# First head, values' turning, weight splits and end of a two-block fp32 kernel put in another order

## The chip, the cores and the metric

The program runs on one core of one Trainium2 chip. A core has engines with instruction queues of their own: TensorE (PE) multiplies, VectorE (DVE), ScalarE (ACT) and GpSimd (POOL) do elementwise work, and SyncE (SP) issues most of the DMAs. They meet only through semaphores. The metric is device microseconds of one execution; the program of before takes 1271.08 us (median of three, 1270.89 to 1271.17). Here a change of less than about 0.2%, 2.54 us, counts as no change.

## What is computed

512 tokens of 1024 channels go through two blocks in fp32. The reference, cut to what matters (`split`, `topk` = 128, norms and short convolutions as named):

```
def first_block(x, ...):
    h = rmsnorm(x, norm_mix_g)
    bg, cg, xv, q, k, v, z, a, b, ga, gb = split(h @ w_in)
    y_a = (bg * causal_dwconv(cg * xv, conv_a_w)) @ w_a_out
    q, k, v = split(silu(causal_dwconv(concat(q, k, v), gdn_conv_w)))      # 8 heads of 128
    q, k = l2norm(q) * 128 ** -0.5, l2norm(k)
    o = gated_delta_rule_chunked(q, k, v, g, beta)                         # chunks of 64, triangular solve
    y_b = (rmsnorm(o) * gdn_norm_g * silu(z)) @ w_b_out
    x = x + (sigmoid(ga) * y_a + sigmoid(gb) * y_b) @ w_o
    x = x + conv_ffn(rmsnorm(x, norm_ffn_g), w_up, ffn_conv_w, w_down)
    return rmsnorm(x, norm_final_g)

def second_block(x, ...):
    z = rmsnorm_2(x, norm_g) @ w_in
    pv, pg, dq, dk, dv, dg, iq, ik, iw, fq, fk, fv, fg, ff = split_columns(z)
    a_out = pool_mixer(pv, pool_w, pool_scale) * silu(pg)
    b_out = dsa_mixer(dq, dk, dv, iq, ik, iw * 8 ** -0.5, topk) * silu(dg) # 6 heads of 64, 128 selected keys
    c_out = fox_mixer(fq, fk, fv, log_sigmoid(ff + fox_bf)) * silu(fg)     # 6 heads of 64, causal
    x = x + concat(a_out, b_out, c_out) @ w_out
    return rmsnorm_2(x, final_g)
```

## The kernel before

**Weights in two parts.** Every large product is made as units of 128 output channels by 512 tokens. A weight tile comes by DMA into `raw` (four buffers), ScalarE rounds it to its high part `whi` (L1329, two buffers), and another engine takes the difference as the low part `wlo` (two buffers). TensorE then runs 24 matmuls of 128x128 by 128x512 into a PSUM bank of `gb`: high by high, low by high, high by low for each of eight k (L833). The low part is made by VectorE in `split` (L1810), except for the units in `POOL_SPLITS`, where GpSimd makes it (L2756). These are units 9 to 21 of the second block's 32 input units (`Z_UNITS`). ScalarE's high part of unit n waits for the end of unit n-2 on TensorE, since `whi` has two buffers, and a unit starts when its low part is there.

**First block, first head.** While the eight units of the first delta-rule head run, TensorE's small steps of that head (triangular inverse, 32x32 and 64x64 blocks) stand between them, and VectorE follows an order written out by hand in `first_head()` (L2149 on). Its pieces are `norm_low(k)` (L2122, low part of the normed input's column block k, which the next head's units use), `split`, `rescale` (L2117), `conv` (L2107, three taps), `shuffles` with GpSimd's elementwise inverse (L1931 on VectorE, L2663 and L2666 on GpSimd), `step` (L2014 to L2026), `place_blocks` (copies of diagonal blocks `Up` and `Tp` into `Ui` and `T64`, L2001 and L2003), `xv_gate` (L2129), `turn_pairs` (L2008) and `query_sums` (L1980, L1981). `T64` is printed as `Yb` by the profile, with which it shares its memory. In later heads ScalarE makes the block copies (L1415).

**Second block.** `schedule()` (L107) is a table: for each of the 32 units and each quarter of a unit it lists the steps that stand beside TensorE's unit on every engine. Six head groups g, each of two heads, start 15 quarters apart, from quarter 28 on. For a group and one of four query tiles: scores on TensorE (L1207), `s` on VectorE (bias and row maximum, L2463), `exp` on ScalarE (L1730), `weigh`, a reciprocal on VectorE (L2471) and a scaling on ScalarE (L1738), then the transposition on TensorE (L1219). After the four tiles come the product with the values (L1229), `pv` (gating, L2486) and `low` (L2492). `turn_v(g)` (L2477) turns the group's values on VectorE; then SyncE sends them out and brings them back, in the units that `V_OUT` lists. Beside all this VectorE runs 48 rounds of the top-k selection (MAX8, L2443, and MATCH_REPLACE8, L2444), on 256, 384 or 512 columns, each query tile's last one ending in L2446, and after each unit `z_out` (L2510). GpSimd also makes the gates (L2738, L2739) and masks (L2728).

**End.** The last 128 tokens are normed in two halves: ScalarE squares (L1786), GpSimd makes the factor (L2765 to L2770), VectorE multiplies both halves by the gain (L2604) as soon as they are there, and when the factor is known VectorE scales half 0 (L2610) and ScalarE half 1 (L1790). Then the output leaves by DMA.

## Time and profile before

| | us |
|---|---|
| median of three runs | 1271.08 |
| profiled execution | 1270.91 |
| its span in the profile | 1269.2 |
| TensorE busy | 1253.5 (99%) |
| VectorE busy | 834.1 (66%) |
| ScalarE busy | 576.9 (45%) |
| GpSimd busy | 223.7 (18%) |

The span is what the profile records from the first to the last instruction; 1.71 us of the profiled execution lie outside it. TensorE has almost no idle time, so a share of busy time says nothing of where a few microseconds could go. What can be read is each single idle stretch of TensorE, who ended it, and what stood in that engine's queue in front. A row of the timeline is: start, duration, engine, line, operation, output and inputs, count, and in brackets the idle time before it and who ended it. Instructions on VectorE are recorded longer than they hold the queue, by the time in which the next one has already begun; where one follows another, the distance of two starts is what an instruction costs.

### The profile page before, as it was taken

Reading aid. Unit: us, or ns where it says so; the run is one execution under the profiler, and the core shown is the slowest. Engines: PE = TensorE matmul, PEld = TensorE weight load, DVE = VectorE, ACT = ScalarE, POOL = GpSimd, SP = SyncE. Lnnn points to the kernel's source line nnn. Section 1 sums busy time; section 2 is a strip of 40 time slices with the busy share of each in tenths; the row PEclk is TensorE's granted clock in tenths of the full one; section 3 lists DMA queues with packets and bytes.
Section 4 is the critical chain, followed back from the end, with each engine's and each line's share of the span. In section 5 each row is a group of like instructions: output and inputs, shape, how many; then the busy total and the mean of one; then the engine's idle time right before and its main releaser. Section 6 shows DMA issues by size and latency. Waiting matters only on the chain.

```text
span 1269.2 us, 20146 instructions
## 1 busy us (share of the span) xinstructions
PE 1253.5 (99%) x6633; PEld 1007.8 (79%) x6633; DVE 834.1 (66%) x1710; ACT 576.9 (45%) x1045; POOL 223.7 (18%) x476
## 2 busy tenths in 40 slices
PE   8999999999999999999999999999999999999998
PEld 6777878878788788888888888888888777777776
DVE  6978768687776853444477773367765687794743
ACT  5564544545454432223344442244445455666632
POOL 2613214032140400001300000000004124440021
PEclk9999999999999999999999999999999999999999
DMA  6245263443534534333233323433224333343221
GB/s 186 76 122 126 83 145 97 122 122 86 141 82 125 132 86 115 99 99 97 87 100 99 95 69 96 120 100 99 80 75 117 102 101 100 87 113 100 83 67 67
DMA packets 283492, 130.01 MB, mean 102 GB/s; under 512 B 77296, under 2 KB 276271, under 8 KB 283445
## 3 DMA queue, kind: packets, MB, share of 16 engines
q1 hardware_dynamic: 283445, 129.42, 37.2%
q8 instruction: 25, 0.41, 0.1%
q14 instruction: 22, 0.18, 0.0%
HBM read 119.34 MB, written 10.06 MB: 102 GB/s over the span
## 4 chain that ended last, share of the span: by engine, by line
PE 90%; DVE 4%; issue 1%; ACT 1%; POOL 0%; DVEq 0%; ACTq 0%
PE gb L833 78%; PE gb L1279 2%; PE gd L1279 1%; PE gd L1229 1%; PE gd L1219 1%; DVE wlo L1810 1%; PE gd L1207 1%; PE gd L1005 1%; PE gd L1016 1%; PE gd L925 0%; PE gd L933 0%; PE gd L994 0%; PE gd L993 0%; PE gd L1012 0%; PE gb L1207 0%
## 5 line engine op out<-in xcount | busy, mean ns | idle before, releaser
L833 PE MATMUL gb<-act_a,whi 128*128 128x512 f32 x2656 | 888.4, 398 | 0.2 <-DVE wlo L1810 0.2
L833 PEld LDWEIGHTS gb<-act_a,whi 128*128 128x128 f32 x2656 | 498.9, 188 | 111.6 <-issue 9.5
L833 PE MATMUL gb<-act_a,wlo 128*128 128x512 f32 x1408 | 549.0, 390 | 0.0
L1810 DVE TENSOR_TENSOR wlo<-raw,whi 128x1024 fp32r<-128x1024 f32 (+1 forms) x197 | 235.6, 1196 | 134.3 <-ACT whi L1329 132.3
L1329 ACT ACTIVATE whi<-raw 128x1024 fp32r<-128x1024 f32 (+1 forms) x210 | 215.9, 1028 | 216.9 <-PE gb L833 191.6
L833 PEld LDWEIGHTS gb<-act_a,wlo 128*128 128x128 f32 x1408 | 265.1, 188 | 48.4 <-issue 0.5
L833 PE MATMUL gb<-act_b,whi 128*128 128x512 f32 x432 | 152.5, 393 | 1.3 <-DVE qc L2107 1.3
L833 PEld LDWEIGHTS gb<-act_b,whi 128*128 128x128 f32 x432 | 81.1, 188 | 18.6 <-DVE qc L2107 1.8
L2711 POOL TENSOR_TENSOR zs<-zs,ca 128x512 f32<-128x512 f32 x3 | 4.2, 1396 | 321.3 <-ACT ca L1332 321.3
L833 PE MATMUL gb<-act_b,wlo 128*128 128x512 f32 x128 | 49.9, 390 | 0.0
L2666 POOL TENSOR_TENSOR Ue<-Ue,elt 128x60 f32<-128x60 f32 (+14 forms) x120 | 45.3, 377 | 9.4
L2663 POOL TENSOR_TENSOR elt<-Ti,Ue 128x60 f32<-128x60 f32 (+14 forms) x120 | 38.0, 316 | 28.4 <-DVE Ti L1931 14.1
L2676 POOL TENSOR_TENSOR rr<-ss,eps_one 128x4 f32<-128x4 f32 x8 | 1.6, 199 | 234.6 <-DVE ss L1995 234.6
L2756 POOL TENSOR_TENSOR wlo<-raw,whi 128x1024 fp32r<-128x1024 f32 x13 | 31.2, 2398 | 23.6 <-ACT whi L1329 23.6
L1424 ACT ACTIVATE ob<-gd,hc 128x128 f32<-128x128 f32 x24 | 8.8, 368 | 54.0 <-DVE Rr L2054 54.0
L2318 DVE TENSOR_TENSOR Yb<-gb,Vt 128x512 f32<-128x512 f32 x22 | 15.2, 691 | 24.9 <-PE gb L833 24.9
L2694 POOL TENSOR_TENSOR zs<-zs,ca 128x512 f32<-128x512 f32 x3 | 5.6, 1856 | 134.3 <-ACT ca L1332 134.3
L2357 DVE TENSOR_TENSOR xT<-xT,gb 128x512 f32 (+1 forms) x16 | 11.0, 687 | 27.0 <-PE gb L833 27.0
L833 PEld LDWEIGHTS gb<-act_b,wlo 128*128 128x128 f32 x128 | 24.1, 188 | 4.5
L2443 DVE MAX8 small<-selb 128x8 f32<-128x256 f32 (+2 forms) x48 | 26.5, 551 | 0.6
L2444 DVE MATCH_REPLACE8 selb<-small,selb 128x256 f32<-128x256 f32 (+2 forms) x48 | 26.0, 543 | 0.0
L2107 DVE SCALAR_TENSOR_TENSOR kc<-gb,hw,kc 128x511 f32<-128x511 f32 (+2 forms) x24 | 18.0, 748 | 7.7 <-ACT kc L1445 7.1
(487 smaller groups left out, 1497.5 us busy)
## 6 DMA issues: line engine op xcount, KB each, us to landing
raw<-in_w_in_dram SPq DMA_DIRECT2D x102, 512.0 KB, 3.5
raw<-in_w_up_dram SPq DMA_DIRECT2D x44, 512.0 KB, 3.5
raw<-in_w_down_dram SPq DMA_DIRECT2D x16, 384.0 KB, 3.1
raw<-in_w_down_dram SPq DMA_DIRECT2D x16, 320.0 KB, 3.1
raw<-in_w_a_out_dram SPq DMA_DIRECT2D x8, 512.0 KB, 3.8
raw<-in_w_b_out_dram SPq DMA_DIRECT2D x8, 512.0 KB, 3.4
raw<-in_w_o_dram SPq DMA_DIRECT2D x8, 512.0 KB, 3.4
raw<-in_w_out_dram SPq DMA_DIRECT2D x8, 512.0 KB, 3.5
```

The costliest lines, as they stand in the source:

```text
L833: ins = pe.matmul(gb[:, b, :], l, r, start=(first and m == 0), stop=(last and m == len(todo) - 1))
L1005: pe.matmul(gd[:, 3, 0:P], Ui[:, c, :], rhs, start=True, stop=True).then_inc(vn_done, 1)
L1279: ins = pe.matmul(place(c, half), l, r, start=False, stop=(i == KD - 1 and m == 2), skip_group_check=True)
L1329: sc.activation(whi[:, i % 2, 0:k * P], raw[:, i % 4, 0:k * P], ACT.Copy).then_inc(hi_ready, 1)
L1810: dve.tensor_tensor(wlo[:, i % 2, 0:k * P], raw[:, i % 4, 0:k * P], whi[:, i % 2, 0:k * P].bitcast(F32), ALU.subtract).then_inc(split_read ...
L2107: ins = dve.scalar_tensor_tensor(dst[:, a:T], gb[:, at, 0:T - a], hw[:, 4 * b + 3 - a:4 * b + 4 - a], dst[:, a:T], ALU.mult, ALU.add)
L2318: dve.tensor_tensor(scaled[s], gb[:, 2 * q + s, :], flat(Vt), ALU.mult).then_inc(up_scaled, 1)
L2443: link(dve.max(small[:, 0:8], v))
L2444: link(dve.match_replace(v, small[:, 0:8], v, TAKEN))
L2663: pool.tensor_tensor(elt[:, :, 0:n], row_at(m), Ue[:, :, m:m + 1].to_broadcast([P, TC, n]), ALU.mult).then_inc(el_used, 1)
L2666: pool.tensor_tensor(Ue[:, :, m + 1:E], Ue[:, :, m + 1:E], elt[:, :, 0:n], ALU.subtract).then_inc(el_done, 1)
L2756: pool.tensor_tensor(wlo[:, n % 2, :], raw[:, n % 4, :], whi[:, n % 2, :].bitcast(F32), ALU.subtract).then_inc(split_ready, 1)
```

## The change

Four things change, and TensorE's own 2185 instructions stay in the same order.

1. First head, VectorE: `norm_low` 0 and 1 no longer stand ahead of the third unit's split and convolution, and all eight stand later than before; `query_sums` moves ahead of `step(13)`; the four copies `Ui<-Up` leave VectorE for ScalarE (`place_blocks`, between `level(14)` and `level(15)`), the two copies of `T64` stay.
2. Second block: `turn_v(g)` for g below 5 stands five quarters of a unit earlier, and the transfers behind it one or two units earlier (`V_OUT`).
3. `POOL_SPLITS` ends six units earlier: the low parts of units 16 to 21 are made by VectorE.
4. End: half 1 is made by one instruction on VectorE when the factor is known (gain and factor together), and ScalarE scales half 0.

```diff
-V_OUT = (13, 17, 21, 25, 28, len(Z_UNITS) + 2)
+V_OUT = (12, 16, 19, 23, 27, len(Z_UNITS) + 2)
...
-        todo.setdefault(start + (7 if g < GROUPS - 1 else 10), []).append((2, ("turn_v", g)))
+        todo.setdefault(start + (2 if g < GROUPS - 1 else 10), []).append((2, ("turn_v", g)))
...
-        POOL_SPLITS = range(N_Z + 9, N_Z + 22)
+        POOL_SPLITS = range(N_Z + 9, N_Z + 16)
...
+            def place_blocks(h):
+
+                sc.wait_ge(t_ready, 3 * h + 2)
+                for b in range(P // B):
+                    ins = sc.activation(Ui[rows(b), :, rows(b)], Up[rows(b), :, :], ACT.Copy)
+                ins.then_inc(ui_ready, 1)
+
...
                 level(14)
+                place_blocks(0)
                 level(15)
...
-            sc.activation(outs[:, TC - 1, T:2 * T], outs[:, TC - 1, T:2 * T], ACT.Copy,
+            sc.activation(outs[:, TC - 1, 0:T], outs[:, TC - 1, 0:T], ACT.Copy,
                           scale=small[:, 36 + TC - 1:36 + TC]).then_inc(outs_ready, 1)
...
                 dve.wait_ge(t_ready, 3 * h + 2)
-                for b in range(P // B):
-                    dve.tensor_copy(Ui[rows(b), :, rows(b)], Up[rows(b), :, :])
                 for b in range(2):
-                    ins = dve.tensor_copy(T64[rows(b), :, rows(b)], Tp[rows(b), :, :])
-                ins.then_inc(ui_ready, 1)
+                    dve.tensor_copy(T64[rows(b), :, rows(b)], Tp[rows(b), :, :])
...
                 shuffles(range(0, 7))
-                norm_low(0)
-                norm_low(1)
                 split(N_B + 5, N_B + 5)
...
                 query_rows(0)
-                norm_low(2)
-                norm_low(3)
+                norm_low(0)
                 step(11, 0)
                 split(N_B + 7, N_B + 7)
                 step(12, 0)
                 rescale(5)
                 turn_values(0)
+                query_sums(0)
                 step(13, 0)
                 place_blocks(0)
                 xv_gate(0)
+                norm_low(1)
+                norm_low(2)
+                turn_pairs(0)
+                norm_low(3)
                 norm_low(4)
-                turn_pairs(0)
-                query_sums(0)
-                norm_low(5)
                 split(N_B + 8, N_B + 8)
                 rescale(6)
                 filter_a(0)
                 bg_in(0)
+                norm_low(5)
                 norm_low(6)
+                first_state(0)
                 norm_low(7)
-                first_state(0)
                 rescale(7)
...
-            for half in range(2):
-                dve.wait_ge(osq, TC + half)
-                ins = dve.tensor_tensor(outs[:, TC - 1, half * T:half * T + T], gd[:, 2 + half, :],
-                                        gfin[:, half * T:half * T + T], ALU.mult)
-                if half == 0:
-                    link(ins)
-            ins.then_inc(outs_ready, 1)
+            dve.wait_ge(osq, TC)
+            dve.tensor_tensor(outs[:, TC - 1, 0:T], gd[:, 2, :], gfin[:, 0:T], ALU.mult).then_inc(outs_ready, 1)
             dve.wait_ge(orr, TC)
-            dve.tensor_scalar(outs[:, TC - 1, 0:T], outs[:, TC - 1, 0:T], small[:, 36 + TC - 1:36 + TC], None,
-                              ALU.mult).then_inc(outs_ready, 1)
+            dve.scalar_tensor_tensor(outs[:, TC - 1, T:2 * T], gd[:, 3, :], small[:, 36 + TC - 1:36 + TC], gfin[:, T:2 * T],
+                                     ALU.mult, ALU.mult).then_inc(outs_ready, 1)
```

Three places show what this does to VectorE's queue. The lines of the changed kernel stand five to eight higher for the same operation (L1810 is L1818, L2107 is L2112, L2477 is L2482). The first place is the first head, ahead of the query's convolution (`qc`). Before:

```order
88 L2122 SCALAR_TENSOR_TENSOR act_a<-Vt,par,act_a 128x512 [waits hn_hi]
89 L2122 SCALAR_TENSOR_TENSOR act_a<-gate,par,act_a 128x512 [waits hn_hi]
90 L1810 TENSOR_TENSOR wlo<-raw,whi 128x1024 [waits hi_ready]
91 L2117 TENSOR_TENSOR gb<-gb,zs 128x512 [waits unit_done,row_kept]
92 L2107 SCALAR_TENSOR_TENSOR qc<-gb,hw,qc 128x511 [waits tap_first,out_scaled]
```

and in the changed kernel:

```order
87 L1939 STREAM_SHUFFLE Ti<-Le 128x36
88 L1818 TENSOR_TENSOR wlo<-raw,whi 128x1024 [waits hi_ready]
89 L2122 TENSOR_TENSOR gb<-gb,zs 128x512 [waits unit_done,row_kept]
90 L2112 SCALAR_TENSOR_TENSOR qc<-gb,hw,qc 128x511 [waits tap_first,out_scaled]
```

Two `norm_low` have left the place in front of the split. The second place is step 13 of the same head and what follows it on VectorE. Before:

```order
121 L1990 STREAM_TRANSPOSE qc<-vc 128x512 [waits conv_silu,out_scaled]
122 L2024 TENSOR_TENSOR Up<-Up,gd 128x4x16 [waits z_done]
123 L2026 STREAM_TRANSPOSE Tp<-Up 128x128 [waits u_ready]
124 L2001 COPY Ui<-Up 32x4x32 [waits t_ready]
125 L2001 COPY Ui<-Up 32x4x32 x3
126 L2003 COPY Yb<-Tp 32x4x32 x2
127 L2129 TENSOR_TENSOR cx<-gb,cx 128x512 [waits cg_copied,unit_done]
128 L2122 SCALAR_TENSOR_TENSOR act_a<-gate,par,act_a 128x512 [waits hn_hi]
129 L2008 STREAM_TRANSPOSE Yb<-Ui 32x4x32 [waits u_ready]
```

and in the changed kernel:

```order
119 L1998 STREAM_TRANSPOSE qc<-vc 128x512 [waits conv_silu,out_scaled]
120 L1988 STREAM_TRANSPOSE Ti<-ob 128x512 [waits el_done,sq_ready]
121 L1989 TENSOR_REDUCE small<-Ti 128x4x4 [waits dve_order]
122 L2029 TENSOR_TENSOR Up<-Up,gd 128x4x16 [waits z_done]
123 L2031 STREAM_TRANSPOSE Tp<-Up 128x128 [waits u_ready]
124 L2009 COPY Yb<-Tp 32x4x32 [waits t_ready]
125 L2009 COPY Yb<-Tp 32x4x32
126 L2134 TENSOR_TENSOR cx<-gb,cx 128x512 [waits cg_copied,unit_done]
127 L2127 SCALAR_TENSOR_TENSOR act_a<-gate,par,act_a 128x512 [waits hn_hi] x2
128 L2013 STREAM_TRANSPOSE Yb<-Ui 32x4x32 [waits u_ready]
```

The sums have moved ahead of the step, four copies are gone, and one `norm_low` more stands ahead of the turning of the pairs. The third place is the second block from unit 16's split on, ahead of the reciprocal of group 2's third tile. Before:

```order
718 L2443 MAX small<-selb 128x8 [waits dve_order]
719 L2444 MATCH_REPLACE selb<-small,selb 128x384 [waits dve_order]
720 L2510 SCALAR_TENSOR_TENSOR vc<-gb,wk 128x512 [waits z_read,ot_ready,unit_done,dve_order]
721 L2471 RECIPROCAL small<-small 128x2 [waits exp_ready]
```

and in the changed kernel:

```order
716 L1818 TENSOR_TENSOR wlo<-raw,whi 128x1024 [waits split_ready,hi_ready,dve_order]
717 L2482 STREAM_TRANSPOSE past_act_b<-vraw 128x512 [waits v_put,z_read]
718 L2448 MAX small<-selb 128x8
719 L2449 MATCH_REPLACE selb<-small,selb 128x384 [waits dve_order]
720 L2515 SCALAR_TENSOR_TENSOR vc<-gb,wk 128x512 [waits z_read,ot_ready,unit_done,dve_order]
721 L2476 RECIPROCAL small<-small 128x2 [waits exp_ready]
```

A split and a turning of values stand ahead of the same reciprocal. From here to unit 21 five more splits and `turn_v(3)` are put in between the rounds in the same way, and the `turn_v(2)` that stood behind L2510 thirteen rows further down is gone from there.

## Rows read from the trace of the kernel before

**Rows 1.** TensorE's waits: engine, line, releaser, us in total, times, longest.

```profile
PE gb L833 <- DVE qc L2107: 1.3, 1, 1.3
PE gd L1219 <- ACT Yb L1738: 1.0, 1, 1.0
PE gd L977 <- issue: 0.5, 1, 0.5
```

**Rows 2.** Busy time, 1120 to 1140: PE, PEld, DVE, ACT, POOL, clock, DMA.

```profile
1120.00:1140.00 20.00, 20.00 (x100) 15.06 (x97) 18.10 (x48) 11.15 (x32) 8.34 (x5) 1.00 0.40 104
```

**Rows 3.** Timeline, VectorE and TensorE around the first long wait of the first head.

```profile
43.66 0.74 DVE L2122 SCALAR_TENSOR_TENSOR act_a<-Vt,par,act_a 128x512 fp32r<-128x512 f32 x1
45.01 1.30 DVE L1810 TENSOR_TENSOR wlo<-raw,whi 128x1024 fp32r<-128x1024 f32 x1
49.33 0.50 PE L833 MATMUL gb<-act_b,whi 128*128 128x512 f32 x1 [1.34 <-DVE qc L2107]
```

**Rows 4.** Timeline around step 13 of the first head, on VectorE, GpSimd and TensorE.

```profile
58.57 5.85 POOL L2649 TENSOR_TENSOR gate<-xT,zs 128x512 f32<-128x512 f32 x4 [2.60 <-DVE Tp L2016]
61.35 0.31 DVE L2026 STREAM_TRANSPOSE Tp<-Up 128x128 f32<-128x128 f32 x1
61.69 3.04 DVE L2001 COPY Ui<-Up 32x128 f32<-32x128 f32 x4
62.53 0.44 PE L960 MATMUL gd<-Tp,LT 32*32 32x32 f32 x16
67.00 0.65 PE L977 MATMUL gd<-Yb,LT 64*64 64x64 f32 x8 [0.50 <-issue]
66.94 0.71 DVE L1980 STREAM_TRANSPOSE Ti<-ob 128x512 f32<-128x512 f32 x1
68.28 0.74 DVE L2122 SCALAR_TENSOR_TENSOR act_a<-gate,par,act_a 128x512 fp32r<-128x512 f32 x1
```

**Rows 5.** Timeline, second head: the same block copies on ScalarE.

```profile
115.17 1.27 ACT L1415 ACTIVATE Ui<-Up 32x128 f32<-32x128 f32 x4 [3.26 <-DVE Tp L2026]
```

**Rows 6.** Timeline, second block: a split on GpSimd, and L2446 on VectorE.

```profile
1064.85 2.40 POOL L2756 TENSOR_TENSOR wlo<-raw,whi 128x1024 fp32r<-128x1024 f32 x1 [1.35 <-ACT whi L1329]
1064.95 2.45 DVE L2446 TENSOR_SCALAR selb<-selb 128x256 f32<-128x256 f32 x1
1104.64 2.32 DVE L2446 TENSOR_SCALAR selb<-selb 128x384 f32<-128x384 f32 x1
1142.67 0.43 DVE L2446 TENSOR_SCALAR selb<-selb 128x512 f32<-128x512 f32 x1
```

**Rows 7.** Timeline, third tiles of groups 1 and 2 (ScalarE, TensorE), and a turning.

```profile
1069.36 0.72 ACT L1738 ACTIVATE qc<-qc,small 128x512 f32<-128x512 f32 x1 [0.53 <-DVE small L2471]
1070.13 0.66 PE L1219 MATMUL gd<-ident,qc 128*128 128x128 f32 x4 [0.44 <-ACT qc L1738]
1094.10 1.05 ACT L1329 ACTIVATE whi<-raw 128x1024 fp32r<-128x1024 f32 x1
1096.58 0.72 ACT L1738 ACTIVATE qc<-qc,small 128x512 f32<-128x512 f32 x1 [0.28 <-DVE small L2471]
1098.57 0.60 PE L1219 MATMUL gd<-ident,qc 128*128 128x128 f32 x4
1107.48 0.70 DVE L2477 STREAM_TRANSPOSE past_act_b<-vraw 128x512 f32<-128x512 f32 x1
1108.11 0.64 DVE L2492 TENSOR_TENSOR act_a<-ca,act_a 128x512 fp32r<-128x512 f32 x1
```

**Rows 8.** Timeline, the last of the changed transpositions, and VectorE's next idle stretch.

```profile
1143.19 0.49 PE L1219 MATMUL gd<-ident,qc 128*128 128x128 f32 x3
1147.32 1.23 DVE L1810 TENSOR_TENSOR wlo<-raw,whi 128x1024 fp32r<-128x1024 f32 x1 [2.31 <-ACT whi L1329]
```

**Rows 9.** Timeline, the end of the kernel.

```profile
1264.63 0.55 POOL L2770 TENSOR_TENSOR small<-small,mhalf 128x1 f32<-128x1 f32 x1
1265.45 0.72 ACT L1790 ACTIVATE gate<-gate,small 128x512 f32<-128x512 f32 x1 [1.35 <-DVE gate L2604]
```

## The prediction, made before the changed kernel was run

> **What bounds the kernel now.** I read the table of busy times first: TensorE is busy 1253.5 of 1269.2 us, so nearly all of the time is matmul work that the change leaves alone. What an edit of this kind can move is TensorE's idle time, so the second view is the list of TensorE's waits. Apart from the start and the end it holds less than 5 us in all. The ones that lie where the change is made are the wait for the query's convolution in the first head (1.3, the timeline has 1.34), the one ahead of L977 in the same head (0.50), and two waits for a `weigh` in the second block (1.0, on `Yb`, and 0.44, on `qc`) [rows 1, 3, 4, 7]. The third view is busy time by stretch: from 1120 to 1140 TensorE is never idle, but VectorE is busy 18.10 of 20 us, while GpSimd has 8.34 [rows 2]. There VectorE does not bound the kernel, yet has hardly any room. The fourth view is the timeline there. All sums are made against the profiled execution, 1270.91; the median, 1271.08, lies 0.17 above it, which is added at the end.
>
> **First head, ahead of the query's convolution.** VectorE's two `norm_low` take from 43.66 to 45.01, 1.35 us, and stand before the split, whose input was there [rows 3]. Without them the split, the rescaling and the three taps come 1.33 earlier (I leave 0.02 for the handover), and of TensorE's wait of 1.34 nothing that matters is left: -1.33. For this the eight `norm_low` are due only when the next head starts, so that they are paid out of VectorE's idle time later; nothing waits for them in this head.
>
> **Step 13.** From here TensorE asks 1.33 earlier for everything: the product L960, at 62.53 before, could start at 61.20. What it needs is VectorE's transposition L2026, which ended at 61.66 [rows 4]. On VectorE one `norm_low` fewer stands ahead, which saves about 0.7, but part of the other gain is lost because the split before it waits for ScalarE's high part, and that comes with TensorE's clock. And `query_sums` are put in: from 66.94 to 68.28, 1.34 us [rows 4]. By my replay of VectorE's queue L2026 ends at 61.35 and TensorE, with the usual small gap, starts 0.22 late. Of the 1.33, 1.11 are left.
>
> **The turning of the pairs.** L977 waited 0.50, until 67.00 [rows 4]. Now VectorE reaches `turn_pairs` without the four copies, 3.04 us, which were that long because GpSimd's four L2649 ran at the same time. It has one `norm_low` more, 0.67, and starts 0.3 earlier. The two copies of `T64` now take over the place beside GpSimd; I give them 1.1 more than without GpSimd, from the same row (a mean of 0.76 each, where the held ones carried it). So the turning comes 3.04 + 0.3 - 0.67 - 1.1 = 1.57 earlier; the wait is gone if it comes 1.11 + 0.50 = 1.61 earlier. Practically it goes: -0.50. ScalarE's four copies take 1.27 in the second head [rows 5] and lie between 62.53 and 67.00, in 4.47 us in which ScalarE has only two short pairs of copies to do; I cost them at nothing. If that cover were gone, at most 1.27 would come back. First head: -1.33 + 0.22 - 0.50 = **-1.61**, of which I leave 0.03 for waits later in the head: -1.58. The ends for this part are -1.84 (both waits gone, no new one) and 0 (the copies on ScalarE and the held copies of `T64` eat it).
>
> Here a page of the Trainium skill has a word: GPSIMD Engine Reference, Specifications, says that VectorE shares its SBUF interfaces with GpSimd and names no other engine. The trace agrees on VectorE's side (3.04 us for four tiny copies); whether ScalarE's copies stay at 1.27 beside L2649 no row of before shows.
>
> **End.** ScalarE's scaling of half 1 started at 1265.45, since it waited for VectorE's L2604 on both halves, and ended at 1266.17. GpSimd's factor was there at 1264.63 + 0.55 = 1265.18 [rows 9]. Now VectorE's instruction on half 1 (0.70 for 128x512 with two inputs) and ScalarE's on half 0 (0.72) both start behind the factor, and the end comes at about 1266.00: -0.17. Bounds: 0, and the whole 0.27 between 1265.18 and 1265.45.
>
> **Second block, the prices.** A split costs GpSimd 2.40 us, VectorE 1.23, of which some 1.15 are its own [rows 6, 8] (records overlap by 0.07, as 1107.48, 0.70 and 1108.11 show [rows 7]). A turning of values is 0.63 in the queue [rows 7]. L2446 took 2.45 and 2.32 while GpSimd had a split and 0.43, on more columns, while it had none [rows 6]: about 1.97 come back at 1104.64, since GpSimd's split there is gone. VectorE's bill from 1094 to 1149 is then 6 x 1.15 - 1.97 = +4.9, plus a wait: unit 16's high part ends only at 1095.15 [rows 7], 0.6 after VectorE would take it up. The turnings 2 and 3 only move inside this stretch.
>
> **Who waits.** A split or turning put in front of a reciprocal (L2471) delays the `weigh` on ScalarE and then TensorE's transposition. The slack is read at each place as the distance of `weigh` and transposition. At the first, group 2's third tile, `weigh` stood at 1096.58 and the transposition at 1098.57, and where TensorE waited it came 0.77 behind (1069.36 and 1070.13): slack 1.22. In front of this reciprocal now stand the split of unit 16 with its wait (1.15 + 0.62) and `turn_v(2)` (0.63), 2.4 in all, so TensorE waits 1.22 [rows 7]. At the next place, 1109.53, VectorE has won back L2446 and the turning that stood there, but carries unit 17's split: the wait of 1.05 becomes 0.60, -0.45. Then, worked out in the same way, each time on the clock that the earlier waits have already moved: the transpositions at 1115.74 (+0.78), 1123.40 (+0.45), 1127.75 (+0.51), 1135.96 (+0.50), 1143.19 (+0.22, [rows 8]) and the score products at 1146.72 (+0.40). VectorE never has a gap in between; after that its idle 2.31 ahead of 1147.32 [rows 8] takes up the rest. Sum for units 16 to 21: 1.22 - 0.45 + 2.86 = **+3.63**. The ends are -1.05 (the old wait gone, no new one) and +5.5 (the whole bill, 4.9 + 0.6, on TensorE).
>
> **Earlier turnings 0 and 1.** `turn_v(1)` now stands ahead of the reciprocal for which TensorE already waited 0.44 [rows 7], so that its 0.63 are paid in full: +0.64 with the handover. `turn_v(0)` delays unit 9's high and low part by as much, where the slack is about 0.5: +0.15. The earlier transfers of `V_OUT` meet no due date that I can find, in SyncE's queue as little as for the weights behind them: 0.
>
> **Sum.** 1270.91 - 1.58 - 0.17 + 3.63 + 0.64 + 0.15 = 1273.58; with 0.17 to the median, **1273.8**. The change trades two waits of the first head for some nine shorter ones in the second block.
>
> **Rivals.**
>
> Rival 1, faster: VectorE has the room. It is busy 66% of the span, and six splits at half of GpSimd's price, with L2446 let go, would fit between the reciprocals if the slack at the transpositions were larger than I read it, so that none of the seven is late and the wait of 1.05 goes as well. It decides at 1098.57: TensorE has no wait there. Time: 1271.08 - 1.58 - 0.17 - 1.05 = 1268.3. For it speaks that only one of eight places had a wait before; against it, VectorE's 18.10 of 20 us [rows 2].
>
> Rival 2, no change: the meeting at 1064.95 ends the other way. L2446 began 0.10 after GpSimd's split, at 1064.85, and was held for 2.0 us [rows 6]; it stands ahead of the very reciprocal that costs TensorE 0.44 and, in the change, 0.63 more. If the moved clock lets VectorE begin first, both go: -1.08, 1272.7. The same size comes out if two of the later delays overlap better than in my serial reckoning. The Trainium skill has this under Advanced Engine Details and Errata, Mode Summary: instructions of GpSimd and two-port instructions of VectorE "will interfere/block eachother". That the blocking goes both ways is the page's; the row shows VectorE's side.
>
> Rival 3, slower still: the first head gives nothing, because the `T64` copies stay held until GpSimd is done, or because ScalarE's copies come late for L977. Then 1273.75 + 1.58 = 1275.3.
>
> Rival 4: half of the bill is hidden, since the serial reckoning puts every delay on TensorE: 1273.75 - 0.5 x 4.42 = 1271.5.
>
> **Chances.** Forecast 0.45, rival 1 0.13, rival 2 0.17, rival 3 0.10, rival 4 0.15. A measurement of this kernel can tell about 0.2% from no change, that is 1268.5 to 1273.6. The forecast lies just above the upper bound; of its 0.45 I put 0.33 above and 0.12 below. With rival 3 and a little of rival 2, slower has 0.44; faster, from rival 1, 0.13; within 0.2%, 0.43. The range leaves out rival 1 and a tail above rival 3: 1269.8 to 1275.4.
>
> **What would show it.** Right: VectorE's split of the first head's third unit starts near 43.7, TensorE's wait for L2107 is gone, a wait of some 0.2 ahead of L960; in the second block a wait of about 1.2 at the transposition near 1098, others of 0.2 to 0.8 up to 1147, and VectorE without a gap from 1105 to 1149; L2446 near 1104 at about 0.4. Wrong: TensorE's busy share of 1080 to 1160 unchanged (rival 1); L2446 near 1065 at 0.4 (rival 2); L977 waiting a microsecond (rival 3). The number would also be off if the high parts of units 16 to 21 came earlier or later than before against TensorE's clock, since each of VectorE's splits waits for one.

## The result

The changed kernel takes 1274.51 us (median of ten, 1274.32 to 1274.67) against 1271.18 for the kernel before in the same runs: +3.33 us, a ratio of 1.0026 with an interval of 1.0018 to 1.0035. It is slower, by a little more than the 0.2% that a measurement can tell (the interval begins just below it). The prediction had 1273.8 and a range of 1269.8 to 1275.4; its sign and its mechanism held, most terms of its sum came out within 0.1 to 0.3 us, and the sum was 0.7 too low.

Both traces record the same 6633 matmuls of TensorE, in the same order. So the start of any one of them can be set against the start of the same one in the trace of before. This difference is called its position below; it counts what the rows of waits leave out.

The list of TensorE's waits of the changed kernel (engine, line, releaser, us in total, times, longest) answers to [rows 1]. L1746 is the changed kernel's `weigh` on ScalarE, L1738 there its `exp`:

```profile
PE gd L1219 <- ACT qc L1746: 2.9, 4, 1.1
PE gd L1219 <- ACT Yb L1746: 1.1, 3, 0.6
...
PE gb L1207 <- ACT zs L1738: 0.4, 1, 0.4
...
PE gd L984 <- ACT Yb L1506: 0.3, 1, 0.3
...
PE gd L1169 <- ACT qc L1721: 0.2, 1, 0.2
```

Both waits of the first head (1.3 on L2107 and 0.5 ahead of L977) are gone from it. The transpositions L1219, which waited twice for 1.5 us in all, now wait seven times for 4.0. The stretch of [rows 2], in the same view (PE, PEld, DVE, ACT, POOL, clock, DMA), with that of 1080 to 1100, where the chain of new waits begins:

```profile
1080.00:1100.00 20.00, 18.90 (x93) 14.42 (x92) 14.85 (x41) 11.67 (x34) 5.76 (x6) 1.00 0.14 34
...
1120.00:1140.00 20.00, 19.32 (x95) 13.42 (x95) 19.07 (x43) 10.38 (x31) 2.78 (x2) 1.00 0.37 96
```

From 1120 to 1140 VectorE is busy for 19.07 of 20 us (18.10 before), GpSimd for 2.78 (8.34), and TensorE, which had no idle time, has 0.68; from 1080 to 1100, where it had none either, it has 1.10. TensorE's clock is 1.00 in these stretches in both kernels. The timeline of the first head, VectorE, GpSimd, ScalarE and TensorE, answers to [rows 3, 4, 5]:

```profile
43.88 1.23 DVE L1818 TENSOR_TENSOR wlo<-raw,whi 128x1024 fp32r<-128x1024 f32 x1
...
56.74 5.85 POOL L2649 TENSOR_TENSOR gate<-xT,zs 128x512 f32<-128x512 f32 x4 [1.94 <-DVE Tp L2021]
...
61.05 0.31 DVE L2031 STREAM_TRANSPOSE Tp<-Up 128x128 f32<-128x128 f32 x1
61.40 1.50 DVE L2009 COPY Yb<-Tp 32x128 f32<-32x128 f32 x2
...
61.51 0.44 PE L960 MATMUL gd<-Tp,LT 32*32 32x32 f32 x16
...
62.56 1.26 ACT L1482 ACTIVATE Ui<-Up 32x128 f32<-32x128 f32 x4
...
64.96 0.30 DVE L2013 STREAM_TRANSPOSE Yb<-Ui 32x128 f32<-32x128 f32 x1
...
65.43 0.67 PE L977 MATMUL gd<-Yb,LT 64*64 64x64 f32 x8
```

The split starts at 43.88 instead of 45.01, L960 at 61.51 instead of 62.53 and L977, without a wait, at 65.43 instead of 67.00. Of the waits of before in the second block one stands in no row above (timeline of TensorE):

```profile
1109.53 0.55 PE L1219 MATMUL gd<-ident,Yb 128*128 128x128 f32 x3 [1.05 <-ACT Yb L1738]
```

In the changed kernel they stand at these places (timeline of TensorE, units 12 to 21; answers to [rows 7, 8]):

```profile
1069.97 0.66 PE L1219 MATMUL gd<-ident,qc 128*128 128x128 f32 x4 [1.01 <-ACT qc L1746]
1099.67 0.55 PE L1219 MATMUL gd<-ident,qc 128*128 128x128 f32 x3 [1.10 <-ACT qc L1746]
1110.25 0.55 PE L1219 MATMUL gd<-ident,Yb 128*128 128x128 f32 x3 [0.61 <-ACT Yb L1746]
1117.22 0.44 PE L1219 MATMUL gd<-ident,qc 128*128 128x128 f32 x2 [0.59 <-ACT qc L1746]
1125.31 0.33 PE L1219 MATMUL gd<-ident,Yb 128*128 128x128 f32 x1 [0.15 <-ACT Yb L1746]
1130.13 0.33 PE L1219 MATMUL gd<-ident,qc 128*128 128x128 f32 x1 [0.24 <-ACT qc L1746]
1138.87 0.44 PE L1219 MATMUL gd<-ident,Yb 128*128 128x128 f32 x2 [0.29 <-ACT Yb L1746]
1150.34 1.14 PE L1207 MATMUL gb<-gate 64*128 64x128 f32 x8 [0.37 <-ACT zs L1738]
```

The transposition at 1098.57 of before, which did not wait, now stands at 1099.67 with 1.10 us of waiting, and six more places follow up to 1150, of which only the first (1110.25, before at 1109.53) waited before. VectorE's side of it, the same stretch:

```profile
1095.11 1.23 DVE L1818 TENSOR_TENSOR wlo<-raw,whi 128x1024 fp32r<-128x1024 f32 x1 [0.74 <-DVE selb L2449]
1096.26 0.70 DVE L2482 STREAM_TRANSPOSE past_act_b<-vraw 128x512 f32<-128x512 f32 x1
...
1105.53 1.23 DVE L1818 TENSOR_TENSOR wlo<-raw,whi 128x1024 fp32r<-128x1024 f32 x1 [1.01 <-ACT whi L1329]
1107.92 0.36 DVE L2451 TENSOR_SCALAR selb<-selb 128x384 f32<-128x384 f32 x1
```

L2451 is L2446 of before: 0.36 instead of 2.32 us, since GpSimd has no split there ([rows 6]). The two splits stand in front of work that could run, for 0.74 and 1.01 us, until ScalarE's high part is there. (The first is put down to VectorE's own L2449, which had been done; what comes at that time is ScalarE's high part.)

### The profile page after: what moved, and what is told of

Read it like the earlier page. It is cut to its first block, busy times and chain, and to the rows that moved or that the text cites. A ratio compares the mean times of both kernels' runs of the same rounds, so it can differ in the third digit from the quotient of the medians.

```text
span 1272.7 us, 20155 instructions
## 1 busy us (share of the span) xinstructions
PE 1255.0 (99%) x6633; PEld 1006.4 (79%) x6633; DVE 837.1 (66%) x1711; ACT 577.6 (45%) x1049; POOL 209.2 (16%) x470
## 4 chain that ended last, share of the span: by engine, by line
PE 92%; DVE 5%; issue 2%; ACT 1%; DMA 0%; DVEq 0%; POOLq 0%; ACTq 0%; POOL 0%
PE gb L833 79%; PE gb L1279 2%; PE gd L1279 1%; PE gd L1229 1%; DVE selb L2449 1%; PE gd L1219 1%; DVE small L2448 1%; DVE wlo L1818 1%; PE gd L1207 1%; PE gd L925 1%; PE gd L933 1%; PE gd L1005 1%; PE gd L1016 1%; ACT whi L1329 0%; PE gd L994 0%
## 5 line engine op out<-in xcount | busy, mean ns | idle before, releaser
L1818 DVE TENSOR_TENSOR wlo<-raw,whi 128x1024 fp32r<-128x1024 f32 (+1 forms) x203 | 242.9, 1197 | 136.1 <-ACT whi L1329 133.1
L2449 DVE MATCH_REPLACE8 selb<-small,selb 128x256 f32<-128x256 f32 (+2 forms) x48 | 26.1, 543 | 0.0
L2738 POOL TENSOR_SCALAR gate<-gate 128x512 f32<-128x512 f32 x5 | 7.8, 1564 | 97.0 <-ACT gate L1686 97.0
L2112 DVE SCALAR_TENSOR_TENSOR kc<-gb,hw,kc 128x511 f32<-128x511 f32 (+2 forms) x24 | 18.0, 748 | 7.7 <-ACT kc L1445 7.1
```

Source lines behind the costliest of these rows:

```text
L1818: dve.tensor_tensor(wlo[:, i % 2, 0:k * P], raw[:, i % 4, 0:k * P], whi[:, i % 2, 0:k * P].bitcast(F32), ALU.subtract).then_inc(split_read ...
L2112: ins = dve.scalar_tensor_tensor(dst[:, a:T], gb[:, at, 0:T - a], hw[:, 4 * b + 3 - a:4 * b + 4 - a], dst[:, a:T], ALU.mult, ALU.add)
L2449: link(dve.match_replace(v, small[:, 0:8], v, TAKEN))
```

## The experiments

The twelve kernels are compared with the kernel before on the same chip. My theory was that of the prediction: VectorE, filled up between 1094 and 1149, makes `weigh` and with it TensorE late. The rivals are that the turnings do the harm, that the first head gives nothing, and later that the price of a split is only its duration.

### Each part alone

The first head's order alone:

> The kernel before with the first head's new order and nothing else. Theory (the first head gains what its waits were): TensorE's wait of 1.34 us on the query's convolution goes, one of about 0.2 comes ahead of L960, the 0.50 ahead of L977 goes; the time is 1.4 to 1.6 us below before, 1269.7. Rival (the first head gives nothing lasting, the gain is taken back by later waits): within 0.3 us of before.

```diff
                 level(14)
+                place_blocks(0)
                 level(15)
...
                 shuffles(range(0, 7))
-                norm_low(0)
-                norm_low(1)
                 split(N_B + 5, N_B + 5)
...
                 turn_values(0)
+                query_sums(0)
                 step(13, 0)
...
```

Measured: 1269.84 (1269.73 to 1270.27) against 1271.16, -1.32 us, ratio 0.9990 (0.9981 to 0.9999). The waits for L2107 and ahead of L977 are gone. Ahead of L960 the trace has no row of a wait, but the positions fall back there by 0.18, which is the 0.2 expected. A new wait of 0.19 stands at 1017, of which more below. The time falls by 0.26 less than the 1.58 of the prediction.

The splits alone:

> The kernel before with the low parts of units 16 to 21 on VectorE and nothing else. Theory (VectorE's unbroken chain from 1105 to 1149 sets TensorE's clock, so its length counts and not where the turnings stand in it): a wait of about 0.6 at group 2's third tile (1098), then the chain with turn_v(2) in it, +3.6 us in all, 1274.8. Rival (most of the loss comes from the earlier turnings, the splits alone fit between the reciprocals): at most +1.5, 1272.7.

```diff
-        POOL_SPLITS = range(N_Z + 9, N_Z + 22)
+        POOL_SPLITS = range(N_Z + 9, N_Z + 16)
```

Measured: 1275.11 (1274.92 to 1275.22), +3.95 us, ratio 1.0031 (1.0019 to 1.0043); expected 1274.8. The splits alone cost more than the whole change, and the rival that puts the loss on the turnings falls. TensorE's waits in this kernel, first two places of the chain:

```profile
1099.49 0.66 PE L1219 MATMUL gd<-ident,qc 128*128 128x128 f32 x4 [0.47 <-ACT qc L1738]
1110.67 0.55 PE L1219 MATMUL gd<-ident,Yb 128*128 128x128 f32 x3 [1.22 <-ACT Yb L1738]
```

Without `turn_v(2)` in front of it the first place waits 0.47 instead of 1.10, and the second, where `turn_v(2)` still stands, 1.22 instead of 0.61. So the 0.6 of this turning only changes its place: here it makes no difference where in VectorE's chain it stands. (For the splits themselves the place does make a difference, see the late splits below.)

The turnings alone:

> The kernel before with turn_v five quarters earlier and the transfers behind it, and nothing else. Theory: +0.28 at group 0's tiles, +0.6 at 1070, nothing at 1098.57 since 0.63 is below the slack of 1.22, and -0.63 at 1109.53, where turn_v(2) no longer stands: +0.25, 1271.4. Rival (turnings earlier relieve VectorE where it is full): 0.6 below before.

```diff
-V_OUT = (13, 17, 21, 25, 28, len(Z_UNITS) + 2)
+V_OUT = (12, 16, 19, 23, 27, len(Z_UNITS) + 2)
...
-        todo.setdefault(start + (7 if g < GROUPS - 1 else 10), []).append((2, ("turn_v", g)))
+        todo.setdefault(start + (2 if g < GROUPS - 1 else 10), []).append((2, ("turn_v", g)))
```

Measured: 1271.46 (1271.35 to 1273.16), +0.30 us, ratio 1.0004 (0.9995 to 1.0013), which is no difference by itself; expected 1271.4. The trace shows the two opposite terms as they were expected:

```profile
1071.19 0.66 PE L1219 MATMUL gd<-ident,qc 128*128 128x128 f32 x4 [1.00 <-ACT qc L1738]
1109.98 0.55 PE L1219 MATMUL gd<-ident,Yb 128*128 128x128 f32 x3 [0.48 <-ACT Yb L1738]
```

The wait of 0.44 has become 1.00, that of 1.05 has become 0.48, and nothing waits near 1098: a turning of 0.63 fits into the slack of 1.22. By position the three places are worth +0.28 (at 1047), +0.57 (at 1070) and -0.61 (at 1109).

First head and end together (the diff cut to one line of each):

> The kernel before with the first head's new order and the new end, and neither the splits nor the turnings. Theory: -1.4 to -1.6 and -0.17 to -0.25 add up, 1269.4 to 1269.6. Rival (the end's gain does not show in the time, since the last DMA is the same): as e1_head.

```diff
+                place_blocks(0)
...
+            dve.scalar_tensor_tensor(outs[:, TC - 1, T:2 * T], gd[:, 3, :], small[:, 36 + TC - 1:36 + TC], gfin[:, T:2 * T],
+                                     ALU.mult, ALU.mult).then_inc(outs_ready, 1)
...
```

Measured: 1269.72 (1269.54 to 1269.89), -1.44 us, ratio 0.9989 (0.9979 to 0.9998). The end gives 0.12 more than the first head alone, near the forecast's 0.17. The difference of 0.12 between two kernels is read from their medians only; it lies inside the intervals.

### Parts taken back

> The changed kernel with GpSimd making the low parts of units 16 to 21 again (first head, turnings and end as changed). Theory: the sum of the parts measured alone, 1269.7 and +0.3, 1270.0; the wait at group 2's third tile (about 1098) is gone, since turn_v(2) alone (0.63) is below the slack there. Rival (turnings and splits are both needed for none of it: the turnings cost by themselves): above 1271.

```diff
-        POOL_SPLITS = range(N_Z + 9, N_Z + 16)
+        POOL_SPLITS = range(N_Z + 9, N_Z + 22)
```

Measured: 1269.97 (1269.66 to 1270.77), ratio 0.9992 (0.9982 to 1.0001); expected 1270.0. Near 1098 nothing waits.

> The changed kernel with turn_v and V_OUT as before (first head, splits and end as changed). Theory: 1269.7 and the +3.9 of the splits alone, 1273.7, so that about 0.8 of the changed kernel's loss belong to the turnings: 0.57 at 1070 and 0.3 at group 0. Rival (the early turn_v(2) is what makes the chain late): below 1272.5.

```diff
-V_OUT = (12, 16, 19, 23, 27, len(Z_UNITS) + 2)
+V_OUT = (13, 17, 21, 25, 28, len(Z_UNITS) + 2)
...
-        todo.setdefault(start + (2 if g < GROUPS - 1 else 10), []).append((2, ("turn_v", g)))
+        todo.setdefault(start + (7 if g < GROUPS - 1 else 10), []).append((2, ("turn_v", g)))
```

Measured: 1273.62 (1273.47 to 1273.79), ratio 1.0019 (1.0010 to 1.0029); expected 1273.7. So the turnings cost 0.30 without the splits and 0.89 with them (1274.51 - 1273.62). The parts alone add up to -1.44 + 0.30 + 3.95 = +2.81, the whole is +3.33: the missing 0.5 is `turn_v(2)`. Without the splits its early place takes 0.6 off the wait at 1109 and costs nothing at 1098 (the position falls by 0.59 there in the kernel without splits, and stays as it is near 1098). With the splits it only moves its share forward: from 1094 to 1151 the position rises by 3.80 with the early turnings and by 3.86 without them.

### What a split on VectorE costs

If GpSimd's split holds L2446 for 2.0 us and VectorE's own costs 1.15, then VectorE should take exactly the two splits that collide, units 12 and 17.

> First head and end as changed, turnings as before, and VectorE makes the low parts of units 12 and 17 alone, the two beside which L2446 was held (2.45 and 2.32 us beside GpSimd's split, 0.43 without); GpSimd keeps the other eleven. Theory (GpSimd's split holds L2446; VectorE pays 1.15 and gets about 2.0 back, twice): L2446 takes 0.3 to 0.4, the wait of 0.44 at 1069 goes and the one of 1.05 at 1109 falls to about 0.2, 1268.4. Rival (VectorE's own split costs as much as the hold, or the hold only moves to another instruction): 1269.5 or more.

```diff
-        POOL_SPLITS = range(N_Z + 9, N_Z + 22)
+        POOL_SPLITS = [N_Z + u for u in range(9, 22) if u not in (12, 17)]
...
                 if n in POOL_SPLITS:
+                    if n > POOL_SPLITS[0] and n - 1 not in POOL_SPLITS:
+                        pool.wait_ge(split_ready, n)
```

> As e7_skip, but VectorE makes the low part of unit 17 alone. Theory: only the wait at 1109 falls, from 1.05 to about 0.2, and the one of 0.44 at 1069 stays: 1268.9. Rival: 1269.5 or more, as there.

It has the same wait of GpSimd, and of the list only 17 is left out:

```diff
-        POOL_SPLITS = range(N_Z + 9, N_Z + 22)
+        POOL_SPLITS = [N_Z + u for u in range(9, 22) if u not in (17,)]
```

Measured: 1269.96 (1269.80 to 1270.13) and 1269.68 (1269.53 to 1269.83), against 1269.72 for first head and end. Neither lies below it by anything that can be told. The expectation of 1268.4 and 1268.9 fell, with the rival's time in its place, and the trace of the first says why (timeline of VectorE and TensorE, unit 17):

```profile
1101.93 0.54 DVE L2449 MATCH_REPLACE8 selb<-small,selb 128x384 f32<-128x384 f32 x1
1103.47 1.23 DVE L1818 TENSOR_TENSOR wlo<-raw,whi 128x1024 fp32r<-128x1024 f32 x1 [1.00 <-DVE selb L2449]
...
1105.86 0.36 DVE L2451 TENSOR_SCALAR selb<-selb 128x384 f32<-128x384 f32 x1
...
1108.79 0.55 PE L1219 MATMUL gd<-ident,Yb 128*128 128x128 f32 x3 [1.23 <-ACT Yb L1746]
```

L2451 is as short as I had said (0.36), but the split stands in VectorE's queue ahead of the last round of the selection and waits 1.00 there for the high part (ScalarE's ends at 1103.38; the row names the instruction in front). The price is 1.00 + 1.15 = 2.15, more than the 1.97 that are saved, and TensorE waits 1.23 instead of 1.05, in both kernels. The first of the two splits, at 1063.86, waits 0.93 in the same way, and TensorE's wait of 0.44 at 1070 is still 0.42. I had counted this wait in the prediction at unit 16 (0.62) and forgotten it here.

The changed kernel with its six splits a quarter of a unit later in the queue tells whether this wait is part of its loss:

> The changed kernel with VectorE's splits of units 16 to 21 a quarter of a unit later in its queue, behind the first quarter's steps. Theory (the price of a split on VectorE is its 1.15 plus the wait for ScalarE's high part, 0.74, 1.01 and 0.39 at units 16, 17 and 20 of the changed kernel, since it stands in the queue ahead of work that could run): these waits go, two splits also stand behind a reciprocal instead of ahead of it; TensorE's wait at 1110 (0.61) is gone and the one at 1100 falls from 1.10 to about 0.4: 1272.1 (1271.6 to 1272.8). Rival (only the 1.15 each count): 1274.2 or more.

```diff
             for u in range(len(Z_UNITS)):
-                if u:
+                late = 16 <= u + 1 <= 21
+                if u and not late:
                     split(N_Z + u + 1, N_Z + u + 1)
                 for m in range(4):
+                    if m == 1 and late:
+                        split(N_Z + u + 1, N_Z + u + 1)
```

Measured: 1272.46 (1272.10 to 1272.83), ratio 1.0011 (1.0001 to 1.0020): 2.05 us less than the changed kernel; expected 1272.1. None of VectorE's six splits waits for its input any more. TensorE's wait at the first place is 0.40, at the second it is gone, and at the third, the second of these rows, it is 0.43 (0.59 in the changed kernel):

```profile
1099.01 0.66 PE L1219 MATMUL gd<-ident,qc 128*128 128x128 f32 x4 [0.40 <-ACT qc L1746]
1115.58 0.44 PE L1219 MATMUL gd<-ident,qc 128*128 128x128 f32 x2 [0.43 <-ACT qc L1746]
```

The splits cost 4.54 us in the changed kernel (1274.51 - 1269.97, the kernel without them), and 2.05 of it came from where they stood in VectorE's queue: ahead of an input that was not there, and ahead of a reciprocal. This kernel moved both at once, and how the 2.05 divide between them was not measured. The rest, 2.49, is the work itself and what else stands in its way.

### What GpSimd's split holds

The other way to free L2446 is to let GpSimd wait. The semaphore that it waits for is one that VectorE raises there in every kernel of this text.

> First head and end as changed, turnings and splits as before; GpSimd waits, ahead of its splits of units 12 and 17, until L2446 of the query tile in question has ended (a semaphore that VectorE raises there). Theory (what makes TensorE wait at 1069 and 1109 is that GpSimd's split, begun 0.1 and 0.3 us earlier, holds L2446 for about 2.0; whoever comes first goes first): L2446 takes 0.3 to 0.4 twice, GpSimd's splits begin some 0.4 to 0.7 later, which nobody waits for, both of TensorE's waits go (0.44 and 1.05): 1269.7 - 1.45 = 1268.3. Rival (GpSimd's later split makes its unit late, or other work of VectorE is held in place of L2446): 1269.5 or more.

```diff
                 if n in POOL_SPLITS:
+                    if n - N_Z in (12, 17):
+                        pool.wait_ge(sel_ready, 1 if n - N_Z == 12 else 2)
                     pool.tensor_tensor(wlo[:, n % 2, :], raw[:, n % 4, :], whi[:, n % 2, :].bitcast(F32),
                                        ALU.subtract).then_inc(split_ready, 1)
```

Measured: 1268.34 (1268.16 to 1269.50) against 1271.13, ratio 0.9980 (0.9971 to 0.9989); expected 1268.3. It is 2.8 us below before, the lowest median here. Against first head and end alone that is 1.4 less; the intervals of the two ratios overlap, but the trace has the gain at the two places: the position falls by 0.65 at 1070 and by 0.73 at 1109. VectorE and GpSimd at the two places, and TensorE at the second:

```profile
1063.85 0.29 DVE L2451 TENSOR_SCALAR selb<-selb 128x256 f32<-128x256 f32 x1
...
1064.30 2.42 POOL L2758 TENSOR_TENSOR wlo<-raw,whi 128x1024 fp32r<-128x1024 f32 x1 [1.89 <-DVE selb L2451]
...
1102.87 0.36 DVE L2451 TENSOR_SCALAR selb<-selb 128x384 f32<-128x384 f32 x1
1103.15 0.68 DVE L2515 SCALAR_TENSOR_TENSOR gate<-gb,wk 128x512 f32<-128x512 f32 x1
1103.75 0.70 DVE L2482 STREAM_TRANSPOSE past_act_b<-vraw 128x512 f32<-128x512 f32 x1
1104.37 1.93 DVE L2497 TENSOR_TENSOR act_a<-ca,act_a 128x512 fp32r<-128x512 f32 x1
...
1103.38 2.38 POOL L2758 TENSOR_TENSOR wlo<-raw,whi 128x1024 fp32r<-128x1024 f32 x1 [3.28 <-DVE selb L2451]
...
1107.09 0.55 PE L1219 MATMUL gd<-ident,Yb 128*128 128x128 f32 x3 [0.38 <-ACT Yb L1746]
```

The wait of 0.44 is gone and that of 1.05 is down to 0.38. What is left is again a hold: beside GpSimd's split L2497 takes 1.93 (0.64 in [rows 7]), while L2515 and L2482 run at their usual 0.68 and 0.70 beside it. L2497 reads two tensors from SBUF, L2482 one, L2515 one and one from PSUM. The Trainium skill has this in GPSIMD Engine Reference, Specifications, where the shared interfaces bring contention with VectorE's two-port modes or its instructions with two SBUF inputs; the trace agrees, with a hold of 1.3 us for the second kind (L2497) and of 2.0 for L2446, which has one SBUF input and so would be of the first; no row shows its mode.

The hold goes both ways, and the one that starts first is not held. Two places of the trace of before show it with the same two instructions, a split on VectorE and L2739 on GpSimd:

```profile
1205.40 1.29 POOL L2739 TENSOR_TENSOR cx<-gate,cx 128x512 f32<-128x512 f32 x1
1206.04 1.72 DVE L1810 TENSOR_TENSOR wlo<-raw,whi 128x1024 fp32r<-128x1024 f32 x1 [1.06 <-ACT whi L1329]
...
1219.00 1.23 DVE L1810 TENSOR_TENSOR wlo<-raw,whi 128x1024 fp32r<-128x1024 f32 x1 [0.26 <-ACT whi L1329]
1219.15 2.22 POOL L2739 TENSOR_TENSOR cx<-gate,cx 128x512 f32<-128x512 f32 x1
```

Where GpSimd begins first it takes 1.29 and VectorE 1.72; where VectorE begins first it takes 1.23 and GpSimd 2.22. The prediction said that the row it had shows VectorE's side only; this pair shows the other.

> As e9_pool_waits, but GpSimd begins unit 17's split only behind VectorE's L2497 (the low part of group 1's product, two SBUF inputs), which that kernel held for 1.93 us instead of 0.65, while L2482 and L2515, each with one SBUF tensor input, ran at their usual 0.70 and 0.68 beside the same split. Theory (GpSimd's split holds VectorE's instructions with two SBUF inputs as well): L2497 takes 0.65, the rest of the wait at 1107 (0.38) goes: 1267.9 to 1268.0. Rival (unit 17's low part is now late, or the wait at 1107 has another cause): 1268.3 or more.

Against the kernel before this one:

```diff
-                    if n - N_Z in (12, 17):
-                        pool.wait_ge(sel_ready, 1 if n - N_Z == 12 else 2)
+                    if n - N_Z == 12:
+                        pool.wait_ge(sel_ready, 1)
+                    if n - N_Z == 17:
+                        pool.wait_ge(m_lo, 2)
```

Measured: 1268.69 (1268.37 to 1269.12), ratio 0.9979 (0.9970 to 0.9988), not to be told from the one before, and above the 1267.9 to 1268.0 of the theory. Theory and rival each name something that happens, and the two cancel:

```profile
1104.15 0.65 DVE L2497 TENSOR_TENSOR act_a<-ca,act_a 128x512 fp32r<-128x512 f32 x1
...
1104.95 2.39 POOL L2760 TENSOR_TENSOR wlo<-raw,whi 128x1024 fp32r<-128x1024 f32 x1 [5.07 <-DVE act_a L2497]
...
1107.48 0.47 PE L833 MATMUL gb<-act_a,whi 128*128 128x512 f32 x1 [0.67 <-POOL wlo L2760]
```

L2497 is back at 0.65 and the transposition does not wait, but GpSimd's split, 1.57 later, ends at 1107.34, and TensorE waits 0.67 for the unit itself. The position falls by 1.28 at the transposition and rises by 0.86 at the unit's first matmul behind it.

### The copies of the first head

> The kernel before with the first head's new order on VectorE, but with the four block copies still on VectorE. Theory (they are held beside GpSimd's L2649, as in before, 3.0 for four, and stand ahead of the turning of the pairs): L977 waits about 1.7 us, 1271.5, so that moving the copies is worth about 1.7 of the first head. Rival (the copies are no longer held, since VectorE comes to them at another time): L977 waits below 0.5, 1270.2. Beside it: the wait of 0.19 at 1017 (L1169 on ScalarE's qc), which stands in each kernel with the new first head and in none without; if it comes from ScalarE's added instructions it is gone here.

Against the kernel with the first head's order alone (ScalarE's `place_blocks` is gone as well):

```diff
                 dve.wait_ge(t_ready, 3 * h + 2)
+                for b in range(P // B):
+                    dve.tensor_copy(Ui[rows(b), :, rows(b)], Up[rows(b), :, :])
                 for b in range(2):
-                    dve.tensor_copy(T64[rows(b), :, rows(b)], Tp[rows(b), :, :])
+                    ins = dve.tensor_copy(T64[rows(b), :, rows(b)], Tp[rows(b), :, :])
+                ins.then_inc(ui_ready, 1)
```

Measured: 1270.25 (1270.11 to 1271.97), ratio 0.9995 (0.9986 to 1.0005). The theory's 1271.5 fell. It is the rival's time, though not quite for its reason: the copies are still held, but for less, and L977 waits 0.85, between the 1.7 of the theory and the 0.5 of the rival (VectorE and TensorE):

```profile
61.27 2.01 DVE L2001 COPY Ui<-Up 32x128 f32<-32x128 f32 x4
63.29 0.45 DVE L2003 COPY Yb<-Tp 32x128 f32<-32x128 f32 x2
...
66.22 0.65 PE L977 MATMUL gd<-Yb,LT 64*64 64x64 f32 x8 [0.85 <-issue]
```

GpSimd's four L2649 start at 56.66 here and end at 62.5, before the last copies. The two copies of `T64` take 0.45 here, behind the four, and 1.50 in the changed kernel, where they come first: of these small copies the ones that VectorE comes to while L2649 is at work are held, be they `Ui` or `T64`. The six take 2.46, the two take 1.50, so ScalarE's four copies free VectorE by about 1.0, and the time by 0.4 (1270.25 - 1269.84). Inside the head they are worth more: at L1005 the position is -0.80 in this kernel and -1.48 in the one with ScalarE's copies. Of these 0.7, 0.3 are given back at 1017.

The new wait of 0.19 at 1017 (L1169, on ScalarE's `qc`) stands in all ten kernels of this text in which ScalarE makes these copies, and this kernel, with the same order otherwise, has none (nor have the two in which the first head is as before). So it comes with moving the copies to ScalarE, 950 us earlier. By TensorE's positions it costs 0.3: 1013.88 of before stands at 1012.55 in the changed kernel, 1018.29 at 1017.26. In the kernel with the first head's order alone ScalarE's next instruction (L1721 on `Yb`) starts 0.37 after the end of the matmuls L1186 that it reads, where it is 0.07 in the kernel before. Whether that comes from the four added instructions themselves or from the earlier time at which this stretch then runs was not separated, and no view names what ScalarE waits for there.

## Why the prediction was right, and where it was off

Right as a whole: slower, 1273.8 against 1274.5 (against the kernel before, +2.7 forecast and +3.3 measured), and by the mechanism that it names, VectorE filled up between 1094 and 1149 and TensorE waiting behind `weigh`. That the result lies above 0.2%, and not on that bound as forecast, is owed to misses: the first head, the end, the early turnings and units 16 to 21 all came out on the side of slower, by 0.3, 0.05, 0.1 and 0.2. By its steps:

- **Query's convolution and turning of the pairs.** The wait of 1.34 and that of 0.50 went. The wait ahead of L960 did not show as a row, but the position falls back there by 0.18 (forecast 0.22). L960 stands 1.02 earlier and L977 1.57, in a run whose start was 0.13 later; without that it is 1.15 and 1.70, forecast 1.11 and 1.61. L984, which waits 0.28 for ScalarE's L1506, gave 0.16 back. At the L1005 that waits (77.27 before, 75.85 now) 1.42 are left, so that the head itself gave 1.55, forecast 1.58. That ScalarE's copies keep their length beside L2649 held: 1.26. So did the 1.1 that the held copies of `T64` were given: 1.50 here, 0.45 where they are not held.
- **First head as a term of the sum.** Mis-sized, -1.32 alone instead of -1.58. What was missing is the 0.3 at 1017, outside the head, which the step "I cost them at nothing" (ScalarE's copies) left out.
- **End.** Forecast -0.17; from the last square on ScalarE to the last result 2.55 us instead of 2.76 in the traces, -0.12 by the medians.
- **Turnings 0 and 1.** Forecast +0.15 and +0.64; the positions show +0.28 (at 1047) and +0.59 (at 1070, from -0.75 to -0.16). The first was too small.
- **Units 16 to 21.** Forecast +3.63; the positions go from -0.15 (1094.22 to 1094.07) to +3.65 (1151.06 to 1154.71), +3.80. Place by place the forecast had +1.22, -0.45, +0.78, +0.45, +0.51, +0.50, +0.22 and +0.40; the positions move by +1.25, -0.38, +0.76, +0.42, +0.48, +0.52, +0.23 and +0.49. The rows of waits are smaller than what TensorE loses (0.59 for the 0.76, none for the 0.23), and a reader who checks the forecast by them alone would call it too high.
- **The high part's wait** was 0.74 at unit 16 (0.6 forecast), 1.01 at unit 17 and 0.39 at unit 20, and apart from the last two VectorE had no gap from 1105 to 1149, as forecast. The prediction names only the first. At the second place the terms that it names (1.05 of old wait, less 1.97 for L2446 and 0.63 for the turning, plus 1.15 for the split) leave no wait at all; with unit 17's 1.01 they give 0.61, which is what was measured. How the prediction came to its 0.60 there it doesn't show. That these waits are a real part of the price the kernels with VectorE's splits of units 12 and 17 show (the wait of 1.05 plus 2.15 less 1.97 is 1.23, as measured), and the late splits fit it.
- **A slip at the first place.** 2.4 less the slack of 1.22 is 1.18, not 1.22.
- **Rival 1** (VectorE has the room) falls with the splits alone, 1275.11. Its time of 1268.3 also leaves out the early turnings, which the forecast has at 0.79. **Rival 2** (L2446 comes first at 1065) did not happen: L2451, as it is called there, took 2.46, and the wait at 1070 is 1.01. Its mechanism is right, though: the kernel in which GpSimd is made to come second gains its 1.4. **Rival 3** falls with the first head alone. **Rival 4** falls: no half was hidden.
- The chance for slower, 0.44, was kept down because 1273.8 lay on the bound of what can be measured.

## What to carry to other kernels

An engine that is 66% busy over the span can be full for the 50 us in which a job is to be given to it: read the busy time by stretch, and for each waiter the slack between what it needs and when it is needed, and put the new job's price against that slack. The price of a job in an in-order queue is its duration plus the time that it stands there waiting for its input; moved behind work that could run, and two of them behind a reciprocal, six splits cost 2.05 us less. Where the start of each instruction can be set against the same one of another trace, the loss is read from the positions and not from the rows of waits. Where GpSimd's long instruction holds a short one of VectorE that TensorE waits for, it can pay to let the long one start later than it could, here by 0.5 and 0.8 us: one semaphore wait at two places gave 1.4 us, as much as the whole new first head.

## What the hardware showed

- Beside GpSimd's split of 128x1024 (2.4 us, two SBUF inputs) VectorE's `TENSOR_SCALAR` on SBUF took 2.45 and 2.32 instead of 0.29 and 0.36, and its `TENSOR_TENSOR` with two SBUF inputs 1.93 instead of 0.65. `STREAM_TRANSPOSE` (0.70) and `SCALAR_TENSOR_TENSOR` with one input in PSUM (0.68) were not held, nor were `MAX8` and `MATCH_REPLACE8` (0.55 and 0.54 on 384 columns, with and without it).
- The one that begins second is held, on either engine: VectorE's split 1.72 instead of 1.23, GpSimd's `TENSOR_TENSOR` of 128x512 2.22 instead of 1.29.
- GpSimd's `TENSOR_SCALAR` of 128x512 (L2738, one input, 1.49) was not seen to hold the same two-input instruction of VectorE: begun 0.5 earlier, at 1160.70 and 1217.58 of before, it left L2492 at 0.69.
- VectorE's tiny copies beside four GpSimd instructions of 128x512 took 1.50 for two or 2.01 for four; ScalarE's four, beside the same, 1.26, as in the second head ([rows 5]).
- A wait of 0.19 on TensorE appeared 950 us behind four copies that were moved to ScalarE, in each kernel that has them there. Its cause is open.
